# GpSimd in place of VectorE for sixteen groups of modulation sums, two instructions for one

## The reference, cut to what matters

```python
s_lat = jax.nn.silu(c)
mod = (s_lat @ ada_w[l] + ada_b[l])[:, None, :]
sh1, sc1, g1, sh2, sc2, g2 = jnp.split(mod, N_MOD, axis=-1)
...
# first block, feed-forward part
h2 = rms_norm(x, g_ff[l])
x = x + jnp.square(jax.nn.relu(h2 @ w_ff1[l])) @ w_ff2[l]
```

## Time and profile before

| | us |
|---|---|
| median of 3 runs | 2590.56 |
| lowest and highest | 2587.63, 2590.9 |
| the profiled execution | 2590.04 |
| its span in the trace | 2588.2 |
| PE busy | 2561.2 (99%) |
| DVE busy | 1923.4 (74%) |
| ACT busy | 1186.2 (46%) |
| POOL busy | 0.2 (0%) |

### The profile page before, as it was taken

How to read it: one execution, slowest core, us unless ns; L and a number is a source line. 1 busy time by engine, 2 the same in 40 slices (tenths; PEclk the granted TensorE clock), 3 DMA queues, 4 the chain that set the end, 5 groups by cost and what they waited for, 6 DMA issues and landing times.

```text
span 2588.2 us, 49739 instructions
## 1 busy us (share of the span) xinstructions
PE 2561.2 (99%) x20824; PEld 2476.9 (96%) x20824; DVE 1923.4 (74%) x2451; ACT 1186.2 (46%) x1263; POOL 0.2 (0%) x4
## 2 busy tenths in 40 slices
PE   9999999999999999999999999999999999999997
PEld 8889999999999999999999899959999999999997
DVE  8888887997998888888892236776666666666667
ACT  7766564445544444444442234343544444444443
POOL 0000000000000000000000000000000000000000
PEclk9999999999999999999999999999999999999999
DMA  8766666767888888888863244424455555555553
GB/s 312 251 242 215 235 242 237 259 244 246 275 277 286 289 285 282 286 289 284 274 226 111 96 167 148 141 75 148 163 196 196 191 191 191 193 196 196 194 190 105
DMA packets 282440, 558.23 MB, mean 216 GB/s; under 512 B 10295, under 2 KB 16728, under 8 KB 281944
## 3 DMA queue, kind: packets, MB, share of 16 engines
q1 hardware_dynamic: 282120, 553.60, 62.7%
q10 hardware_dynamic: 144, 2.10, 0.2%
HBM read 553.56 MB, written 2.10 MB: 215 GB/s over the span
## 4 chain that ended last, share of the span: by engine, by line
PE 92%; DVE 5%; issue 1%; DMA 1%; ACT 1%; SPq 0%; DVEq 0%; ACTq 0%
PE PS L1738 78%; PE PS L1752 3%; PE PS L1749 3%; PE PS L1751 3%; DVE WL L952 2%; PE PS L2074 1%; PE PS L2085 1%; PE PS L1981 1%; PE PS L2092 1%; DVE adac L1369 0%; DMA adab<-in_ada_w 0%; DMA X<-in_x 0%; DVE X L1330 0%; DVE ada1c L1211 0%; ACT WH L511 0%
## 5 line engine op out<-in xcount | busy, mean ns | idle before, releaser
L511 ACT ACTIVATE WH<-RAW 128x1024 fp32r<-128x1024 f32 x840 | 887.8, 1060 | 1267.2 <-PE PS L1738 1146.1
L952 DVE TENSOR_TENSOR WL<-RAW,WH 128x1024 fp32r<-128x1024 f32 x840 | 1017.2, 1223 | 574.8 <-ACT WH L511 565.9
L1738 PE MATMUL PS<-XL,WH 128*128 128x256 f32 x4288 | 664.9, 277 | 0.0
L1738 PE MATMUL PS<-XH,WH 128*128 128x256 f32 x3752 | 587.5, 279 | 2.1 <-ACT WH L511 1.6
L1738 PEld LDWEIGHTS PS<-XL,WH 128*128 128x128 f32 x4288 | 569.6, 188 | 0.0
L1738 PEld LDWEIGHTS PS<-XH,WH 128*128 128x128 f32 x3752 | 499.3, 188 | 5.0 <-issue 2.9
L1738 PE MATMUL PS<-XH,WL 128*128 128x256 f32 x3752 | 503.9, 277 | 0.0
L1738 PEld LDWEIGHTS PS<-XH,WL 128*128 128x128 f32 x3752 | 462.1, 188 | 0.0
L1738 PE MATMUL PS<-HH,WH 128*128 128x256 f32 x1728 | 268.2, 277 | 2.6 <-DVE X L1330 1.7
L1738 PE MATMUL PS<-HL,WH 128*128 128x256 f32 x1728 | 266.1, 276 | 0.0
L1738 PEld LDWEIGHTS PS<-HH,WH 128*128 128x128 f32 x1728 | 228.2, 188 | 3.7 <-DVE X L1330 2.7
(11 more groups left out here) (275 smaller groups left out, 1900.1 us busy)
## 6 DMA issues: line engine op xcount, KB each, us to landing
RAW<-in_w_ff SPq DMA_DIRECT2D x128, 1024.0 KB, 5.8
RAW<-in_w_in SPq DMA_DIRECT2D x111, 1024.0 KB, 5.0
RAW<-in_w_up SPq DMA_DIRECT2D x88, 1024.0 KB, 4.8
adab<-in_ada_w SPq DMA_DIRECT2D x128, 512.0 KB, 5.2
RAW<-in_w_down SPq DMA_DIRECT2D x44, 1024.0 KB, 5.0
ada1b<-in_ada_w SPq DMA_DIRECT2D x64, 512.0 KB, 6.0
RAW<-in_w_out SPq DMA_DIRECT2D x32, 1024.0 KB, 5.1
RAW<-in_w_oa SPq DMA_DIRECT2D x8, 1024.0 KB, 5.2
```

Source lines behind the costliest of these rows:

```text
L511: A(WH[:, c.base % 2, hs], RAW[:, c.base % SLOTS, hs], ACT.Copy).then_inc(hi_done, 1)
L952: tt(WL[:, b, hs], RAW[:, c.base % SLOTS, hs], WH[:, b, hs].bitcast(f32), ALU.subtract)\
L1738: ins = MM(out[:, f, :], w[:, b, kk, f * P:(f + 1) * P], x, start=first and not low and n == 0 and f % 2 == 0, stop=last and low, skip_gro ...
```

## The change

`add_piece` is taken out of DVE's program and written into POOL's, with a loop that runs over all sixteen groups. GpSimd does the piece in two instructions where VectorE had one: it multiplies the weights in place (`w = w * x`), and adds them to the accumulator (`acc = acc + w`). Each waits for the one before it by a semaphore; `ada_mul` is new. SP's loads, PE's transposes and their waits stay as they are.

```diff
-            def add_piece(a, n, order):
-
-                dve.wait_ge(ada_in[order.base % 2], order.turns(2, 1, 16))
-                if n == 0:
-                    dve.wait_ge(sm["mt_done"], a.value(1, -1))
-                for m in range(2):
-                    if order.base or m or order.i is not None:
-                        dve.wait_ge(ada_acc, order.value(2, m - 1) if order.since(1) else m)
-                    acc = adac[:, a.base % 2, m, :]
-                    w, x = adab[:, order.base % 2, m, :], ctmp[:, 0, 2 * n + m:2 * n + m + 1]
-                    ins = ts(acc, w, x, None, ALU.mult) if n == 0 else stt(acc, w, x, acc, ALU.mult, ALU.add)
-                    ins.then_inc(ada_acc, 1)
-                if n == 7:
-                    dve.wait_ge(ada_acc, order.value(2, 2))
-                    acc = adac[:, a.base % 2, :, :]
-                    tt(acc[:, 0, :], acc[:, 0, :], acc[:, 1, :], ALU.add).then_inc(ada_sum, 1)
...
-                    add_piece(a, s, Place(8 * j.base + s, j.i, 8 * j.per))
...
-                for n in range(16):
-                    if ADA_TAIL[n] == s:
-                        add_piece(Place(ADA_GROUPS - 2 + n // 8), n % 8, Place(8 * (STEPS1 - 2) + n))
...
+        @block.gpsimd
+        def _(pool):
+            G = nc.gpsimd
+
+            def add_piece(a, n, order):
+
+                pool.wait_ge(ada_in[order.base % 2], order.turns(2, 1, 16))
+                if n == 0:
+                    pool.wait_ge(sm["mt_done"], a.value(1, -1))
+                for m in range(2):
+                    if order.base or m or order.i is not None:
+                        pool.wait_ge(ada_acc, order.value(2, m - 1) if order.since(1) else m)
+                    acc = adac[:, a.base % 2, m, :]
+                    w, x = adab[:, order.base % 2, m, :], ctmp[:, 0, 2 * n + m:2 * n + m + 1]
+                    if n == 0:
+                        ins = G.tensor_scalar(acc, w, x, None, ALU.mult)
+                    else:
+                        G.tensor_scalar(w, w, x, None, ALU.mult).then_inc(ada_mul, 1)
+                        pool.wait_ge(ada_mul, a.plus(-ADA_GATE).value(14, 2 * n + m - 1))
+                        ins = G.tensor_tensor(acc, acc, w, ALU.add)
+                    ins.then_inc(ada_acc, 1)
+                if n == 7:
+                    pool.wait_ge(ada_acc, order.value(2, 2))
+                    acc = adac[:, a.base % 2, :, :]
+                    G.tensor_tensor(acc[:, 0, :], acc[:, 0, :], acc[:, 1, :], ALU.add).then_inc(ada_sum, 1)
...
+            pool.wait_ge(sm["csil_done"], 1)
+            for j in range(2 + 2 * FF1_ITERS):
+                ff1_step(Place(j))
+            for n in range(16):
+                add_piece(Place(ADA_GROUPS - 2 + n // 8), n % 8, Place(8 * (STEPS1 - 2) + n))
```

More of the change, by code:

```diff
@@ L324, in build_program @@
         ada_acc = sem("ada_acc")
+        ada_mul = sem("ada_mul")
         ada_sum = sem("ada_sum")
@@ L1716, in _, with ff1_step @@
                 scaled(NT, quarter(X, n), lambda k: col("final", k), n)
+        @block.gpsimd
[21 more added lines that the diff above has]
+                    G.tensor_tensor(acc[:, 0, :], acc[:, 0, :], acc[:, 1, :], ALU.add).then_inc(ada_sum, 1)
+            def ff1_step(j):
+                _, _, a = ff1_place(j)
+                for s in range(STEP1):
+                    add_piece(a, s, Place(8 * j.base + s, j.i, 8 * j.per))
+            pool.wait_ge(sm["csil_done"], 1)
[3 more added lines that the diff above has]
+                add_piece(Place(ADA_GROUPS - 2 + n // 8), n % 8, Place(8 * (STEPS1 - 2) + n))
         @block.tensor
```

## The result

The changed kernel takes 2830.45 us (median of 4 runs, 2826.27 to 2834.91), against 2589.28 us before: 1.0931 times as long, 95% interval 1.0918 to 1.0944, or 241 us slower. The forecast of a slower kernel held and the time lies inside the range, but 100 us above the 2730 that I named.

The account below looks back on a forecast made before the run. PE was taken as the bound before, POOL through blocking after. POOL's lateness of 116 us in the loop plus 86 - 49 - 14 in the tail gave 139 us, on 2590.04: forecast 2730 us, range 2586 to 2850.

Parts of the forecast that it names:

- What bounds the kernel, and the prize: PE, busy 99% of the span, sets the end; relief of DVE gives back at most 5.2 us, counted as 0.
- The price of POOL's instructions: For a group on POOL, 16 products at 0.75 us and 15 additions at 1.22 us: 30.3 us.
- the estimate beside my sum: POOL's work for a group by the GPSIMD Engine Reference: 15 x 1.36 + 16 x 0.77 = 32.7 us.
- The handoffs: Each of POOL's 31 instructions for a group waits 0.12 us for its predecessor's semaphore: 3.7 us.
- The blocking: POOL stands still for DVE's instructions with two SBUF inputs: 17 for a step at 1.1 us, 18.7 us.
- The loop: Fourteen groups on POOL at 52.7 us take 738 us, where before they had 622: POOL falls 116 us behind.
- The slack of 18 us: In the loop a tile's load has 10.7 us of slack before ACT and 6.9 behind it, together 18 us.
- the sum that gave 139 us: PE's total lateness after loop and tail: 116 + 86 - 49 - 14 = 139 us.
- The 98 us that I named for PE: PE's lateness at the end of the loop: 116 - 18 = 98 us.
- The tail: POOL's last pieces need 59.5 us and 26 us of blocking, together 86 us, against 49 before.
- The slack of 14 us: In the tail, the next stage's tile loads behind the last piece load may be 14 us late before PE waits.
- The signs that I named: Product 0.75, addition 1.22, group 52.7 us; `WL` longer or delayed; SP's wait for `adac` largest; ACT waiting for `RAW`, PE for `WH`.

Follow-up runs that it names:

- experiment 6: Changed kernel with every piece and the joining addition cut to one column on GpSimd, waits and loads kept: 2581.55 us against 2589.31 for the kernel before.
- experiment 1: Changed kernel with DVE's `WL` subtraction done for one column only, POOL's instructions unchanged: 2632.91 us, beside 2588.05 for the kernel before.
- Experiment 3: Changed kernel split in two: only the loop's fourteen groups on GpSimd, 2787.03 us; only the tail's sixteen pieces there, 2632.04 us; kernel before 2589.95.
- experiments 2 and 5: 2: changed kernel without POOL's 14 additions for a group, 2590.49 us. 5: each piece divided, accumulator 0 on VectorE, accumulator 1 on GpSimd, 2602.62 us.

## Why the prediction was right, and where its sum was off

**What bounds the kernel, and the prize.** Right: PE was the bound and the relief small. But I had put the most it could give at 5.2 us, the waits of PE that name DVE, and it is 7.8 (experiment 6): this bound did not hold.

**The price of POOL's instructions.** The addition was nearly right, 1.26 to 1.29 us against 1.22, which was also my upper bound. The product was the term that was mis-sized: I took 0.75 us from VectorE's fused row, and it is 1.55, outside my bounds of 0.48 to 1.22 too. With 16 products this is 12.8 us for a group. I had bounded another engine's instruction by the form that is cheap on VectorE; on GpSimd the product with a scalar is dearer than the addition of two tensors (1.55 against 1.26 us), the other way round than on VectorE (0.48 against 0.69). The GPSIMD Engine Reference of the Trainium skill (Performance versus the Vector engine) times a loop over 512 elements at 0.77 us in the best case; taken for this product, as in the estimate beside my sum, the measurement decides against that too.

**The handoffs.** 3.7 us for 31. The records of the chain without blocking sum up to 16 x 1.55 + 15 x 1.26 = 43.7 us, and experiment 1 has 46.1, with some blocking by `HL` and the context norm left. So the handoffs are at most 2.4 us.

**The blocking.** Right in kind. I had 18.7 us for a group; experiment 1 shows 12.8. DVE carries a share of the hold itself, 0.49 us for each `WL`, and half of the products are not held up at all. That this accounts for the whole difference is not shown.

**The loop.** My 52.7 us for a group came out as 58.9: the product's +12.8 less 5.9 for the blocking and 1.3 for the handoffs, which I had both put too high. That the errors went against each other is luck; with the product alone mis-sized the group would have stood at 65.5. POOL ends 824 - 622 = 202 us late in place of 116.

**The slack of 18 us.** It was there in the loop. The tile of the earlier trace rows, found by counting the tiles, in the kernel after on SP, ACT, DVE and PE:

```profile
1121.82 0.37 SPq L350 DMA_DIRECT2D RAW<-in_w_ff  x1
...
1127.66 2.01 ACT L512 ACTIVATE WH<-RAW 128x1024 fp32r<-128x1024 f32 x2 [3.90 <-DMA RAW<-in_w_ff]
...
1128.75 2.36 DVE L953 TENSOR_TENSOR WL<-RAW,WH 128x1024 fp32r<-128x1024 f32 x2 [2.66 <-ACT WH L512]
...
1131.03 1.22 DVE L1318 SCALAR_TENSOR_TENSOR FR<-PS,rt 128x1024 f32<-128x1024 f32 x1
1132.38 0.74 PE L1755 MATMUL PS<-HH,WH 128*128 128x256 f32 x4 [2.06 <-DVE FR L1318]
```

It is asked for 116.9 us later than before (1004.96) and used 102.9 us later (1029.44), so 14.0 us of slack were used up. The tile before it, asked for at 999.09 and used at 1024.00 in the kernel before, comes 116.5 and 98.9 us late: 17.6 us. What the reasoning had missed is the 4 us between them. I followed one tile from its DMA to its matmul, but DVE takes its instructions in the order written, and `FR` and the `X` additions stand behind the `WL` of tiles that are not there yet. Here both `WL` are made, then `FR`, and PE starts 0.13 us after its end. Over the stage PE waited 131 us for `FR` and `X`, and 41 for `WH`.

In the tail most of the slack is gone, and there the reading of the rows failed. I had read 10.7 us before ACT from a tile of the steady step. In the tail the kernel before asks for its tiles late itself (SP, then ACT, of the kernel before):

```profile
1272.76 0.42 SPq L349 DMA_DIRECT2D RAW<-in_w_ff  x1
...
1281.37 1.06 ACT L511 ACTIVATE WH<-RAW 128x1024 fp32r<-128x1024 f32 x1 [2.42 <-DMA RAW<-in_w_ff]
```

ACT already waits for this tile: nothing is left before it. In the kernel after the tile is asked for 212.8 us later and used 203.7 us later, 9 us of slack. The last transpose in the loop (1260.80 us before) is 181.6 us late, the one of the group before the tail (1283.13) 197.9, when POOL is 201.9 late.

The 18 us are no term of the sum that gave 139 us, though; they only divide it between loop and tail. So their failure in the tail moved no part of the forecast time. The 98 us that I named for PE at the end of the loop were 182.

**The tail.** POOL needs 96 us for fourteen pieces where I had 86 (the last piece load goes out at 1562.64). The slack of 14 us, which is a term of the sum, was too large: the last loads go out 249.1 us late, PE's first matmul of the next stage comes 240.9 us late (1575.61 against 1334.69), and by the last transpose (1605.62 against 1359.83), behind PE's waits for the squares of the norm, it is 245.8. Some 4 of the 14 us are left in the end. Experiment 3 has 42 us for the tail alone, and I had named 40 for PE in the tail; but by my sum the tail alone, with no lateness from the loop, is 86 - 49 - 14 = 23 us, so this agreement is chance.

The sum by what was measured is 202 + 96 - 49 - 4 = 245 us, the difference of the two profiled executions (2834.91 and 2590.04); the medians differ by 241. Of the 106 us by which it exceeds my 139, 86 are the loop, 10 the pieces of the tail and 10 the slack of 14 us.

**The signs that I named.** The wait of SP for POOL (its largest between 600 and 1600 us), the longer `WL` and ACT's wait for `RAW` were all there. The one for PE was named wrong: I said `WH`, and it was mostly `FR` and `X`.

## What to carry to other kernels

Before work goes to an engine off the critical path, compare the length of its whole chain, with what the neighbour's two-input instructions add, with the period of the stage; and look at whose queue waits for it. Here a chain of 58.9 us beside a period of 43.5 held up the DMA queue of everything else, while with some 33 us of work or less (experiments 2 and 5) the same blocking cost nothing in the steady steps. Read the slack of a tile's way in every stretch that the delay will reach: here it was 14 to 18 us in the loop and 9 or less in the tail, where the kernel before was already short of it. And look at what else the engine in the middle has to do behind the late tile, such as freeing accumulators.

## What the runs showed of the hardware

- On GpSimd, on 128x512 float32, the product with a scalar for each partition takes 1.55 us at its shortest, with a constant 1.48, as a two-input product with the scalar broadcast 1.03, and the addition of two tensors 1.26. I had not expected the one-input form to be the dearest.
- The hold is mutual. With `WL` at full size POOL's product averages 2.25 us (1.58 without) and `WL` 1.72 in the steady part (1.22 before); an instruction of DVE with one input in PSUM keeps its time, 1.21 against 1.22. The hold comes in steps: a product takes about 1.55, 2.5 or 3.6 us.
- TensorE's granted clock, 0.999 of full speed before, is 0.971 over the span of the kernel after. In the steady part it lies between 0.90 and 0.95 for each 100 us, where PE now stands idle for some 15 to 20% of the time, and in the tail it falls to 0.80. So for part of that time PE ran at the lower of its two levels, 1.2 GHz. No run here separates what this added. In the loop POOL's period sets the pace and PE has idle time, so little of it should show there; that is an argument and not a measurement, and for the tail it is open.
